# Three edits to a one-core transformer kernel: the last square of a norm added by VectorE, both tiles of a convolution in step, an output gate tile moved behind the pool projection

## Chip, cores and metric

The kernel runs on one core of one Trainium2 chip. The metric is the device time of one execution in microseconds; lower is better. The engines are called as in the profile: PE (TensorE), DVE (VectorE), ACT (ScalarE), POOL (GpSimd) and SP (SyncE, which here only issues the weight transfers).

## The reference, cut to what matters

A first block runs twice over 512 tokens of width 1024: a norm, one wide projection, a Fourier mix and a retention of four heads, then a feed-forward part with a convolution. A second block follows once, with a context of 256 tokens of its own (`xc`). Its parts in the order of the reference:

```python
x  = ada_out(x,  swiglu(ada_in(x,  mod,  0, norm_pre[0]), ffn_w_in[0], ffn_w_out[0]), mod,  0, norm_post[0], 0.5)
xc = ada_out(xc, swiglu(ada_in(xc, modc, 0, norm_pre[0]), ffn_w_in[0], ffn_w_out[0]), modc, 0, norm_post[0], 0.5)
p  = ada_in(x,  mod,  1, norm_pre[1]) @ w_in        # u, v, output gate, gates, pool
pc = ada_in(xc, modc, 1, norm_pre[1]) @ w_in[:, :M_COLS]
u = silu(short_conv(p[..., :512], conv_w, conv_b))  # three taps along the tokens
h_lat, h_ctx = mlstm_bidir(...)                     # q, k from u by head; chunks of 128; both directions
mix = concat([mlstm_out(h_lat, output_gate, head_norm), pool_mixer(p[..., M_COLS:], pool_w, pool_scale)])
x = ada_out(x, mix @ w_out, mod, 1, norm_post[1], 1.0)
x = ada_out(x, swiglu(ada_in(x, mod, 2, ...), ...), mod, 2, norm_post[2], 0.5)
```

Each `ada_in`, `ada_out`, the closing norm of the first block and each retention head hold an RMS norm: the mean of squares over the 1024 (or 256) features, plus eps, to the power -1/2, times the values. `mlstm_out` multiplies by the sigmoid of the output gate, `pool_mixer` subtracts a group of the pool projection from its moving mean and multiplies by a 128x128 weight.

## The kernel before

Activations lie with the features on the 128 partitions and the tokens along the free axis: a tile of `x` is 128x512, one of the context 128x256, eight tiles (`t` = 0 to 7) make the width. Every product in full precision is three matmuls of halves (`L400` high by high, `L401` low by high, `L402` high by low), so both operands need a high and a low part. ACT makes the high part (`high`, L1087: a copy that rounds), DVE the low one (`low` L1671 or `low_of` L1675: value minus high part).

**Weights** come in chunks of 128x1024 (eight 128x128 blocks). SP brings a chunk to `stage`, ACT makes `WH` (L1067), DVE makes `WL` (L1629), PE uses the eight blocks. `weights(name)` on ACT and DVE makes the chunks up to two beyond the one that `name` uses; `WH` and `WL` have three buffers, and the `WH` of a chunk waits until PE has finished the chunk three before it. A block is three matmuls.

**Norms.** ACT squares a tile (`square`, L1097 for the first into `SSQ`, L1100 for the others into `SCR`), DVE (or POOL for some norms) adds each square to `SSQ` (`add_square`, L1684), and PE sums over the partitions by `rms_first`: four tiny matmuls for 512 tokens from `SSQ` (L500) and four from the last square, which nobody has added, from `SCR` (L504). The records count a 4-byte matmul of this kind as two instructions, so that the trace shows x8. DVE adds eps (L1692), POOL takes the power (L2321), `rms_last` on PE spreads the result over the partitions (L510), and DVE multiplies (L1705), with ACT and DVE making high and low parts of the product.

**Order.** Each engine's program is one list written by hand, and engines wait for each other by semaphores. Some work is written as generators "behind" a linear layer: after every block of a long linear layer each engine calls `walk.tick()`, and `walk.pace` says how many calls make one step of the generator (`yield` to `yield`). In the output gate stage (`og`, four tiles of 128 output features, one chunk each) and in the one that follows (`v2x`, eight) the steps are given by hand: `BESIDE_OG` and `BESIDE_V2`.

**The second block's middle**, in the order of PE: `swiglu` of the context, first half (`c,0`), and of `x` first half, then the second half of the context (`c,1`, 2328 to 2438 us, with the norms `("ao",0,0)` and `("an",1,0)` behind it), output gates (`og`), the value projection `v2x`, the convolution's input `uc` (four heads; the context tile `uc` is 256 tokens, the `x` tile `ux` 512), gates, `v2c`, the pool projection `pu`, then `pool_mean(g)` (a 512x512 matrix of means), `pool_out(g)` and `q_and_k(h, which)`, and `scores(0,0)`. For the convolution ACT scales and adds the bias (`Identity`, L1447), DVE adds the two outer taps (L2157, L2160), ACT takes silu (L1450) and the high part, DVE the low part. DVE also makes `gates_sum`, `gates_maximum` and `gates_order` (L2120 to L2136) between heads.

## Time and profile before

| | |
|---|---|
| median of 3 runs (lowest, highest) | 3179.95 us (3179.87, 3182.98) |
| profiled execution: its own time, span | 3180.08 us, 3178.3 us |
| PE busy, share of the span, matmuls | 3069.9 us, 97%, 14914 |
| DVE busy | 1778.7 us, 56% |
| ACT busy | 1125.9 us, 35% |
| POOL busy | 144.8 us, 5% |
| mean granted clock of PE | 0.987 |
| weight transfers to `stage` | 533 of 512 KB, 3.3 us to landing each |

The profile is of one execution; a row's time is from the span's start. The granted clock is a share of full speed: 1.00 is 2.4 GHz and 0.50 is 1.2 GHz. A wait in brackets is the idle time of that engine just before the instruction, with what released it.

### The profile page before, as it was taken

How to read it: one execution, taken by the hardware profiler on the slowest of the kernel's cores; microseconds unless marked ns; L12 is line 12 of the kernel's file. 1: busy time of each engine (PE TensorE's matmuls, PEld its weight loads, DVE VectorE, ACT ScalarE, POOL GpSimd, SP SyncE). 2: the span in 40 equal slices, each digit the busy share in tenths (PEclk: the TensorE clock that was granted, in tenths of full speed). 3: DMA queues.
4: the chain of work that ended last, by engine and by line, in shares of the span. 5: the costliest groups of instructions: out<-in, count | busy, mean ns of one | idle time of the engine just before them, and what ended most of it. 6: DMA issues, size and time to landing. Idle time of an engine off the chain costs nothing. (4 is left out here: it accounts for less than half of the span.)

```text
span 3178.3 us, 36249 instructions
## 1 busy us (share of the span) xinstructions
PE 3069.9 (97%) x14914; PEld 2569.4 (81%) x14914; DVE 1778.7 (56%) x2524; ACT 1125.9 (35%) x1644; POOL 144.8 (5%) x129
## 2 busy tenths in 40 slices
PE   7999999999999999999999999999999989899998
PEld 5888888888778888888888889888898756778886
DVE  6566656766767566656755555323366655353234
ACT  3323332442324232333433434222234446332221
POOL 0001000000000001100000000000010004100000
PEclk9999999999999999999999999999999989999999
DMA  7354446443343343345322334222344130122221
GB/s 260 126 173 157 155 137 193 133 152 128 126 138 100 126 131 113 112 150 175 118 101 94 100 121 162 95 100 93 99 133 135 67 119 1 54 67 99 98 95 67
DMA packets 106916, 381.73 MB, mean 120 GB/s; under 512 B 11868, under 2 KB 13276, under 8 KB 106752
## 3 DMA queue, kind: packets, MB, share of 16 engines
q1 hardware_dynamic: 82992, 294.41, 27.8%
q10 hardware_dynamic: 23760, 85.01, 8.1%
q8 instruction: 118, 1.93, 0.2%
q14 instruction: 46, 0.38, 0.0%
HBM read 377.28 MB, written 2.10 MB: 119 GB/s over the span
## 5 line engine op out<-in xcount | busy, mean ns | idle before, releaser
L1629 DVE TENSOR_TENSOR WL<-stage,WH 128x1024 fp32r<-128x1024 f32 x533 | 655.8, 1234 | 674.7 <-ACT WH L1067 674.3
L400 PE MATMUL ps<-HH,WH 128*128 128x512 f32 x2188 | 858.1, 392 | 14.8 <-DVE HL L1671 5.8
L401 PE MATMUL ps<-HL,WH 128*128 128x512 f32 x2188 | 853.7, 390 | 0.0
L402 PE MATMUL ps<-HH,WL 128*128 128x512 f32 x2188 | 853.3, 390 | 0.0
L1067 ACT ACTIVATE WH<-stage 128x1024 fp32r<-128x1024 f32 x533 | 557.0, 1050 | 334.5 <-PE ps L402 325.5
L400 PE MATMUL ps<-GH,WH 128*128 128x512 f32 (+1 forms) x1652 | 587.5, 356 | 11.7 <-DVE WL L1629 5.7
L401 PE MATMUL ps<-GL,WH 128*128 128x512 f32 (+1 forms) x1652 | 584.9, 354 | 0.0
L402 PE MATMUL ps<-GH,WL 128*128 128x512 f32 (+1 forms) x1652 | 584.7, 354 | 0.0
L400 PEld LDWEIGHTS ps<-HH,WH 128*128 128x128 f32 x2188 | 412.3, 188 | 103.4 <-issue 8.3
L402 PEld LDWEIGHTS ps<-HH,WL 128*128 128x128 f32 x2188 | 412.0, 188 | 86.5
L401 PEld LDWEIGHTS ps<-HL,WH 128*128 128x128 f32 x2188 | 412.4, 188 | 82.4
L1087 ACT ACTIVATE GH<-SCR 128x512 fp32r<-128x512 f32 (+5 forms) x310 | 165.9, 551 | 700.9 <-DVE SCR L2041 232.9
L400 PEld LDWEIGHTS ps<-GH,WH 128*128 128x128 f32 x1652 | 313.5, 190 | 61.0 <-issue 7.1
L401 PEld LDWEIGHTS ps<-GL,WH 128*128 128x128 f32 x1652 | 313.6, 190 | 43.8
L402 PEld LDWEIGHTS ps<-GH,WL 128*128 128x128 f32 x1652 | 313.4, 190 | 43.0
L1671 DVE TENSOR_TENSOR GL<-SCR,GH 128x512 fp32r<-128x512 f32 (+1 forms) x214 | 133.1, 628 | 127.5 <-ACT GH L1087 127.5
L1656 DVE CUSTOM_DVE_ANT_0 MST<-MST,CB,PAR 128x1024 f32<-128x1024 f32 x158 | 201.9, 1279 | 0.9 <-ACT CB L1389 0.8
L2321 POOL TENSOR_TENSOR V<-V,HM 128x4 f32<-128x4 f32 (+1 forms) x26 | 30.1, 1156 | 2165.4 <-DVE V L1692 2165.4
L2340 POOL TENSOR_TENSOR GL<-SCR,GH 128x512 fp32r<-128x512 f32 (+3 forms) x80 | 89.8, 1145 | 771.2 <-ACT GH L1087 771.0
L2041 DVE TENSOR_TENSOR SCR<-ps,SCR 128x512 f32<-128x512 f32 (+1 forms) x66 | 39.6, 600 | 116.8 <-PE ps L402 112.0
L400 PE MATMUL ps<-WH,HH 128*128 128x256 f32 (+1 forms) x320 | 98.8, 309 | 4.0 <-DVE SCR L1837 4.0
L402 PE MATMUL ps<-WH,HL 128*128 128x256 f32 (+1 forms) x320 | 97.4, 304 | 0.0
(210 smaller groups left out, 2774.1 us busy)
## 6 DMA issues: line engine op xcount, KB each, us to landing
stage<-ws SPq DMA_DIRECT2D x533, 512.0 KB, 3.3
MST<-wm ACTq DMA_DIRECT2D x154, 512.0 KB, 3.3
Z<-wm SPq DMA_DIRECT2D x10, 512.0 KB, 6.8
TAB<-consts ACTq DMA_DIRECT2D x7, 448.0 KB, 3.5
MST<-wm SPq DMA_DIRECT2D x6, 512.0 KB, 6.3
out<-X SPq DMA_DIRECT2D x8, 256.0 KB, 2.1
X<-xT ACTq DMA_DIRECT2D x4, 256.0 KB, 5.4
X<-xT SPq DMA_DIRECT2D x4, 256.0 KB, 6.5
```

Of the source, the lines that this page charges most:

```text
L400: e.matmul(o, wh, mh, start=start, stop=False)
L401: e.matmul(o, wh, ml, start=False, stop=False)
L402: return e.matmul(o, wl, mh, start=False, stop=stop)
L1067: e.activation(wh, src, ACT.Copy).then_inc(whi.sem, whi.up(("w", i)))
L1087: e.activation(dst, src, ACT.Identity if "bias" in more else ACT.Copy, **more).then_inc(hi.sem, hi.up(name))
L1629: e.tensor_tensor(wl, src, wh.bitcast(F32), ALU.subtract).then_inc(wlo.sem, wlo.up(("w", i)))
L1656: e.tensor_tensor_reduce(out=products, in0=a, in1=b, scale=1.0, scalar=res if i else bias, op0=ALU.mult, op1=ALU.add, accum_out=res).then_inc(
L1671: e.tensor_tensor(dst, src, high_part.bitcast(F32), ALU.subtract).then_inc(lo.sem, lo.up(name))
L2041: made(e.tensor_tensor(T, bank("sb", who, half, jj)[:, 0:n], T, ALU.mult), "sb", who, half, jj)
L2321: e.tensor_tensor(V4[:, 4:4 + nt], V4[:, 0:nt], HM[:, 0:nt], ALU.pow).then_inc(power.sem, power.up((k,)))
L2340: e.tensor_tensor(dst, src, high_part.bitcast(F32), ALU.subtract).then_inc(plo.sem, plo.up(name))
```

## The change

1. **Last square by VectorE.** For every norm that is not in the new set `IN_TURN` (three heads of the retention in each of the two layers, and seven norms of the second block and its entry: 13 in all) the last square is also added to `SSQ` by the adding engine, and PE sums `SSQ` alone: one set of tiny matmuls in place of two. For `("an",0,0)` POOL adds it, for the others DVE.
2. **Steps.** Each generator of a norm has one more `yield`, `walk.pace` goes from (2, 3) to (3, 4), and `BESIDE_OG` and `BESIDE_V2` change.
3. **An output gate tile moved.** The fourth `og` tile, with its weight chunk and its sigmoid, stands behind the pool projection. `q_and_k(0, 0)` comes ahead of the first pool mean, and each `pool_out` one mean later. The blocks around it fall into chunks differently: there are 535 chunks, not 533; ACT also loads its table twice more (sigmoid, then exp).
4. **Convolution in step.** Both tiles of a head go through each step together: two `Identity`, then the taps of both, then silu and high part of both, then both low parts; the gates' steps on DVE stand behind the taps.

```diff
 
+                if k not in IN_TURN:
+                    pe.wait_ge(*added_by(k, last))
+                    stat_free()
+                    for t in range(n // 128):
+                        inst = e.matmul(STAT[:, t:t + 1], SSQ[:, t * 128:t * 128 + 128], OC[:, oc:oc + 1], start=True, stop=True)
+                    done(inst, ("ss", k))
+                    return
                 pe.wait_ge(*(added_by(k, last - 1) if last > 1 else (sq, "sq", k, 0)))
...
                 walk.need("mod", 0, 3 * j + 1)
+                yield
                 warm(alone)
                 rms_first(k, n, 0, 7)
...
             walk.behind.append(closing_norm())
-            walk.pace = (2, 3)
+            walk.pace = (3, 4)
...
             pe.wait_ge(lo, "h", ("an", 1, 0), 7)
-            for h in range(NH):
+
+            def output_gate(h):
                 p = take_bank(("og", h), ev, "og", h)
                 lin(("og", h), 8, lambda k: ("w_in2", 0, k * 128, 1024 + h * 128), hx, p[:, :], bg=False)
+
+            for h in range(3):
+                output_gate(h)
                 for _ in range(BESIDE_OG[h]):
                     walk.advance()
 
...
                     running_max(0, k // 2 - 2)
-            close()
+
+            output_gate(3)
 
             qk_w = {}
...
 
             pe.wait_ge(lo, "u", 3, 1)
             pe.wait_ge(lo, "v2", 1)
+            q_and_k(0, 0, score_bank("qk", 0, 0))
+            close()
             pool_mean(0)
-            q_and_k(0, 0, score_bank("qk", 0, 0))
-            pool_out(0)
             q_and_k(0, 1, score_bank("qk", 0, 1))
             q_and_k(0, 2, score_bank("qk", 0, 2))
             pool_mean(1)
+            pool_out(0)
+            pool_mean(2)
             pool_out(1)
-            pool_mean(2)
             pool_mean(3)
             pool_out(2)
             scores(0, 0)
...
                 else:
-                    T = take(("sq", k, t), *((mm, "ss", k) if t == (1 if k[0] == "r" else 7) else added_by(k, t)))
+                    T = take(("sq", k, t), *((mm, "ss", k) if k in IN_TURN and t == (1 if k[0] == "r" else 7) else added_by(k, t)))
...
             for h in range(NH):
                 weights(("uc", h))
-                for part, (name, n, a) in enumerate((("ux", S, h * 768 + 256), ("uc", C, h * 768))):
+                parts = (("ux", S, h * 768 + 256), ("uc", C, h * 768))
+                for part, (name, n, a) in enumerate(parts):
                     T = take((name, h), lo, "u", h, part)[:, 0:n]
                     act.wait_ge(mm, "uc", h)
                     e.activation(T, bank(name, h)[:, 0:n], ACT.Identity, scale=par("cw2", 4 + h),
                                  bias=par("cb2", h)).then_inc(ev.sem, ev.up((name, h)))
+                for part, (name, n, a) in enumerate(parts):
+                    T = SA(name, h)[:, 0:n]
                     act.wait_ge(dv, name, h)
                     e.activation(T, T, ACT.Silu).then_inc(ev.sem, ev.up(("silu", h, part)))
                     act.wait_ge(ev, "silu", h, part)
...
+
+            def last_square(k, n):
+                if k not in IN_TURN and added_by(k, 7)[0] is ssq:
+                    add_square(k, 7, n)
 
...
                         made(e.tensor_tensor(T, bank("y", l, h, t)[:, :], T, ALU.mult), "y", l, h, t)
+                    if h + 1 < NH:
+                        add_square(("r", l, h), 1, S)
 
...
             for h in range(NH):
                 weights(("uc", h))
-                if h == 1:
-                    gates_sum()
-                elif h == 2:
-                    gates_maximum()
-                elif h == 3:
-                    gates_order()
-                for part, (name, n, a) in enumerate((("ux", S, h * 768 + 256), ("uc", C, h * 768))):
+                parts = (("ux", S, h * 768 + 256), ("uc", C, h * 768))
+                for part, (name, n, a) in enumerate(parts):
                     T, p = SA(name, h), bank(name, h)
                     dve.wait_ge(ev, name, h)
                     made(e.scalar_tensor_tensor(out=T[:, 1:n], in0=p[:, 0:n - 1], scalar=par("cw2", h), in1=T[:, 1:n],
...
                     made(e.scalar_tensor_tensor(out=T[:, 0:n - 1], in0=p[:, 1:n], scalar=par("cw2", 8 + h), in1=T[:, 0:n - 1],
                                                 op0=ALU.mult, op1=ALU.add), name, h)
+                if h == 1:
+                    gates_sum()
+                elif h == 2:
+                    gates_maximum()
+                elif h == 3:
+                    gates_order()
+                for part, (name, n, a) in enumerate(parts):
+                    T = SA(name, h)
                     low(UL[:, a:a + n], T[:, 0:n], UH[:, a:a + n], "u", h, part)
             gates_last()
...
             root(("fin",), S)
-            for t in range(1, DT - 1, 2):
+            for t in range(1, DT, 2):
...
 
-        BESIDE_OG = [1, 1, 4, 4]
-        BESIDE_V2 = [1, 0, 1, 2, 2, 2, 1, 1]
+        BESIDE_OG = [2, 4, 5]
+        BESIDE_V2 = [1, 1, 1, 2, 2, 2, 1, 1]
         NORMS = [("n1", 0), *[("r", 0, h) for h in range(NH)], ("n2", 0),
                  ("n1", 1), *[("r", 1, h) for h in range(NH)], ("n2", 1),
                  ("an", 0, 1), ("fin",), ("an", 0, 0), ("ao", 0, 0), ("an", 1, 0), ("ao", 0, 1), ("an", 1, 1),
                  *[("hn", h) for h in range(NH)], ("ao", 1, 0), ("an", 2, 0), ("ao", 2, 0)]
+
+        IN_TURN = {("n1", 0), ("n1", 1), ("n2", 0), ("n2", 1), ("ao", 1, 0), ("an", 2, 0), ("ao", 2, 0),
+                   ("r", 0, NH - 1), ("r", 1, NH - 1)}
         FIRST_SQUARE = {k: before for before, k in zip(NORMS, NORMS[1:])}
         SLOTS_FREE = {("c", 0): ("dn", 1, 1, 7), ("x", 0): ("sd", "c", 0, 7), ("x", 1): ("sd", "x", 0, 7),
                       ("c", 1): ("sd", "x", 1, 7), ("y", 0): ("sum", 3, 5, 1), ("y", 1): ("sd", "y", 0, 7)}
```

(left out: the same edits of `closing_norm`, `ada_in` and `ada_out` for ACT and DVE, where the DVE version calls `last_square(k, n)` ahead of the new `yield`; and the reordering of the pool stage on ACT and DVE, which is that of PE.)

**DVE in the convolution.** DVE's rows of the head `h` = 1, first before, then of the changed kernel (L1629 is L1657 there, L2157 and L2160 are L2192 and L2195, L1671 is L1699; GT are the gates). 128x511 are the taps of `ux`, 128x255 those of `uc`.

```order
L1629 TENSOR_TENSOR WL<-stage,WH 128x1024
L2120 SCALAR_TENSOR_TENSOR GT<-GT 36x768
L2122 SCALAR_TENSOR_TENSOR GT<-GT 36x768
L2157 SCALAR_TENSOR_TENSOR SCR<-ps,PAR,SCR 128x511
L2160 SCALAR_TENSOR_TENSOR SCR<-ps,PAR,SCR 128x511
L1671 TENSOR_TENSOR GL<-SCR,GH 128x512
L2157 SCALAR_TENSOR_TENSOR SCR<-ps,PAR,SCR 128x255
L2160 SCALAR_TENSOR_TENSOR SCR<-ps,PAR,SCR 128x255
L1671 TENSOR_TENSOR GL<-SCR,GH 128x256
```

```order
L1657 TENSOR_TENSOR WL<-stage,WH 128x1024
L2192 SCALAR_TENSOR_TENSOR SCR<-ps,PAR,SCR 128x511
L2195 SCALAR_TENSOR_TENSOR SCR<-ps,PAR,SCR 128x511
L2192 SCALAR_TENSOR_TENSOR SCR<-ps,PAR,SCR 128x255
L2195 SCALAR_TENSOR_TENSOR SCR<-ps,PAR,SCR 128x255
L2160 SCALAR_TENSOR_TENSOR GT<-GT 36x768
L2162 SCALAR_TENSOR_TENSOR GT<-GT 36x768
L1699 TENSOR_TENSOR GL<-SCR,GH 128x512
L1699 TENSOR_TENSOR GL<-SCR,GH 128x256
```

The four taps now follow the weight chunk directly, the two gate instructions stand between them and the low parts, and the two low parts are last.

**ACT in the output gate stage.** Z<-ps is the sigmoid of an `og` tile, SCR<-TAB a square of the context for `("an",1,1)`, WH a weight chunk; before, then changed (L1423 is L1440 there, L1067 is L1083, L1097 and L1100 are L1113 and L1116).

```order
L1423 ACTIVATE Z<-ps 128x512
L1067 ACTIVATE WH<-stage 128x1024
L1423 ACTIVATE Z<-ps 128x512
L1067 ACTIVATE WH<-stage 128x1024
L1097 ACTIVATE SSQ<-TAB 128x256
L1100 ACTIVATE SCR<-TAB 128x256 x2
L1423 ACTIVATE Z<-ps 128x512
L1067 ACTIVATE WH<-stage 128x1024
L1100 ACTIVATE SCR<-TAB 128x256 x5
L1423 ACTIVATE Z<-ps 128x512
L1067 ACTIVATE WH<-stage 128x1024 x2
```

```order
L1440 ACTIVATE Z<-ps 128x512
L1083 ACTIVATE WH<-stage 128x1024
L1113 ACTIVATE SSQ<-TAB 128x256
L1116 ACTIVATE SCR<-TAB 128x256
L1440 ACTIVATE Z<-ps 128x512
L1083 ACTIVATE WH<-stage 128x1024
L1116 ACTIVATE SCR<-TAB 128x256 x6
L1440 ACTIVATE Z<-ps 128x512
L1083 ACTIVATE WH<-stage 128x1024 x2
```

The same eight squares stand one output gate tile earlier, since there are three tiles and not four.

**ACT in the pool stage**, from the high parts of the pool projection on. HH<-ps with PAR is a pool output, HH<-ps without it a pool mean, the single GH<-ps are parts of q and k; before, then changed.

```order
L1087 ACTIVATE GH<-ps 128x512 x4
L1067 ACTIVATE WH<-stage 128x1024 x2
L1087 ACTIVATE HH<-ps 128x512
L1067 ACTIVATE WH<-stage 128x1024
L1087 ACTIVATE GH<-ps 128x512
L1087 ACTIVATE HH<-ps,PAR 128x512
L1087 ACTIVATE GH<-ps 128x512
L1087 ACTIVATE GH<-ps 128x256
```

```order
L1103 ACTIVATE GH<-ps 128x512 x4
L1083 ACTIVATE WH<-stage 128x1024
L1440 ACT_TABLE_LOAD
L1440 ACTIVATE Z<-ps 128x512
L1083 ACTIVATE WH<-stage 128x1024
L1103 ACTIVATE GH<-ps 128x512
L1083 ACTIVATE WH<-stage 128x1024 x2
L1103 ACTIVATE HH<-ps 128x512
L1083 ACTIVATE WH<-stage 128x1024
L1103 ACTIVATE GH<-ps 128x512
L1103 ACTIVATE GH<-ps 128x256
```

A table load, the sigmoid of the fourth output gate tile and the first part of q stand ahead of the first pool mean; the first pool output is no longer between the parts of q and k.

## Rows read from the trace of the kernel before

**Rows 1.** Busy time by engine in four stages of the second block

```profile
core 0: us, PE busy (x) PEld busy (x) DVE busy (x) ACT busy (x) POOL busy (x), PEclk, DMA share, GB/s
2328.00:2438.00 110.00, 100.94 (x807) 99.63 (x806) 77.08 (x104) 50.56 (x76) 9.27 (x6) 0.96 0.47 156
...
2496.00:2561.00 65.00, 55.35 (x271) 45.95 (x270) 40.40 (x58) 28.99 (x41) 0.00 (x0) 0.89 0.21 72
...
2613.00:2720.00 107.00, 93.97 (x459) 62.08 (x458) 57.21 (x120) 64.31 (x147) 50.20 (x51) 0.95 0.01 2
...
2580.36:2612.63 32.27, 22.80 (x76) 16.61 (x76) 22.67 (x28) 21.34 (x31) 0.00 (x0) 0.84 0.49 157
```

**Rows 2.** Timeline of PE: waits in these stages, wait in brackets

```profile
start us, us, engine line op out<-in xcount [idle before <-releaser]
2376.89 1.02 PE L500 MATMUL ps<-OC,SSQ 128*128 128x1 f32 x8 [1.84 <-DVE SSQ L1684]
...
2438.16 0.79 PE L400 MATMUL ps<-HH,WH 128*128 128x512 f32 x1 [4.71 <-DVE HL L1675]
...
2536.01 0.79 PE L400 MATMUL ps<-WH,GH 128*128 128x512 f32 x1 [4.29 <-DVE WL L1629]
...
2546.86 0.80 PE L400 MATMUL ps<-WH,GH 128*128 128x512 f32 x1 [5.36 <-DVE WL L1629]
...
2583.77 0.77 PE L400 MATMUL ps<-WH,GH 128*128 128x512 f32 x1 [3.41 <-DVE GL L1671]
```

**Rows 3.** Same view as rows 1, short stretches; and one wait elsewhere

```profile
2378.00:2384.80 6.80, 6.80 (x34) 6.80 (x34) 3.44 (x6) 1.43 (x3) 1.02 (x1) 0.50 0.40 124
...
2535.00:2541.80 6.80, 5.49 (x12) 3.80 (x12) 5.33 (x9) 2.08 (x4) 0.00 (x0) 0.50 0.24 77
...
2582.80:2589.60 6.80, 5.83 (x14) 4.66 (x15) 3.08 (x4) 1.99 (x3) 0.00 (x0) 0.50 0.24 77
...
891.00:904.00 13.00, 9.63 (x43) 7.68 (x42) 10.30 (x17) 4.11 (x5) 0.00 (x0) 1.00 0.52 170
...
894.73 0.51 PE L400 MATMUL ps<-GH,WH 128*128 128x512 f32 x1 [3.37 <-DVE GL L1671]
```

**Rows 4.** Timeline of PE and DVE around the norm of a retention head

```profile
288.35 0.95 PE L500 MATMUL ps<-OC,SSQ 128*128 128x1 f32 x8
289.17 1.03 PE L504 MATMUL ps<-OC,SCR 128*128 128x1 f32 x8
290.06 0.36 PE L400 MATMUL ps<-WH,HH 128*128 128x256 f32 x1
...
284.45 1.28 DVE L1874 TENSOR_TENSOR SCR<-ps,SCR 128x512 f32<-128x512 f32 x2
285.77 1.23 DVE L1629 TENSOR_TENSOR WL<-stage,WH 128x1024 fp32r<-128x1024 f32 x1
289.70 1.22 DVE L1629 TENSOR_TENSOR WL<-stage,WH 128x1024 fp32r<-128x1024 f32 x1 [2.71 <-ACT WH L1067]
```

**Rows 5.** One head of the convolution: engines, and a wait of ACT

```profile
2524.60:2534.74 10.14, 7.12 (x38) 5.78 (x36) 7.22 (x10) 4.17 (x8) 0.00 (x0) 1.00 0.16 52
...
2519.78 0.63 ACT L1450 ACTIVATE SCR<-SCR 128x512 f32<-128x512 f32 x1 [4.70 <-DVE SCR L2160]
```

**Rows 6.** Timeline of ACT, DVE, PE at the output gate stage's end

```profile
2465.93 1.04 ACT L1067 ACTIVATE WH<-stage 128x1024 fp32r<-128x1024 f32 x1
...
2465.27 0.42 DVE L1684 TENSOR_TENSOR SSQ<-SSQ,SCR 128x256 f32<-128x256 f32 x1 [0.20 <-ACT SCR L1100]
2467.01 1.22 DVE L1629 TENSOR_TENSOR WL<-stage,WH 128x1024 fp32r<-128x1024 f32 x1 [1.31 <-ACT WH L1067]
...
2466.39 0.50 PE L500 MATMUL ps<-OC,SSQ 128*128 128x1 f32 x4
```

**Rows 7.** Timeline of ACT: a table load and what follows

```profile
2501.53 1.28 ACT L1438 ACT_TABLE_LOAD   x1
2502.83 0.84 ACT L1438 ACTIVATE GT<-GT 36x768 f32<-36x768 f32 x1
```

## Prediction before the run

> **What bounds the kernel now.** I read the windows by stage first. PE is busy for 97% of the span (front table), so an edit gains only where PE stands idle, runs at half clock, or has instructions taken away. The stages that the change touches hold much of such time [rows 1]: 9.1 us idle in the context's second half (`c,1`, 110.00 less 100.94), 9.7 in the convolution (65.00 less 55.35), 9.5 in the 32.27 us from the end of the pool projection to the first scores, 13.0 in the head stage behind it. The granted clock there is 0.96, 0.89, 0.84 and 0.95, where the span's mean is 0.987. PE's timeline shows five waits and their releasers [rows 2]: 1.84 us for the last added square, 4.71 for the low part of `h` ahead of the output gates, 4.29 and 5.36 for `WL` chunks in and behind the convolution, 3.41 for the low parts of the pool projection. Behind such waits stand 6.8 us at 0.50 clock, with PE busy 6.80, 5.49 and 5.83 us in three of them [rows 3]. At half clock half of that work is lost time: 3.4, 2.7 and 2.9 us. A wait does not always bring that: one of 3.37 us elsewhere lies in a stretch at 1.00 [rows 3].
>
> **Last square, retention heads.** Between two starts the second set of tiny matmuls takes 290.06 - 289.17 = 0.89 us of a PE that never waits there [rows 4]. Six heads: +5.3 us. In exchange DVE makes six adds of 0.64 us (half of the 1.28 for two tensor operations of that size). The add comes directly behind L1874, which ends at 285.73, so it is done near 286.4, and PE wants it at 288.35: 1.9 us of cover. `WL` behind it slides by 0.64 us; DVE then idles 2.71 us before the next chunk, so nothing else moves. Bounds: 4.9 to 5.3.
>
> **Last square elsewhere.** The closing norm saves the same 0.89, the context's `("an",0,1)`, with half the matmuls, 0.4: +1.3 (0.9 to 1.3). The other norms stand in stages that DVE and ACT chain, below.
>
> **`c,1`.** The 1.84 us wait for the sum, the second set, and the half clock of 3.4 us behind it [rows 2, 3] could together give 6. But from there to 2438 PE goes at the pace of the squares, affines and `WL` on DVE (77.08 us busy of 110.00), and the 4.71 us wait at the end is for the last of the affines: what PE wins early it waits longer there. The extra `yield`, the new pace and one more add on DVE pull steps together by some blocks and no more. Bounds 0 and +6; I take +2.5, nearer to none because the end wait stands.
>
> **Output gates and `v2x`.** With three tiles in place of four the same eight squares of the context lie one tile (24 products) earlier on PE, and the sum of `("an",1,1)` needs the last of them added by DVE. Before, the add of t = 6 ended at 2465.69, PE came at 2466.39 and did not wait [rows 6]. After, PE's sum comes about 3 us earlier, near 2463.3 in the old time, and DVE's add of t = 7 is queued behind the `WL` whose `WH` comes behind the third sigmoid. In the old time that ends near 2466.1, with the `WH` duration of 1.04 and `WL` of 1.22: a new wait of 2.8 us, less 1.1 for steps taken earlier, and a half-clock stretch worth up to 3.4, of which I take 2.0 by the two cases of rows 3. Together -3.7 (bounds -5.5 and 0, where the clock stays and the wait is covered).
>
> **Convolution.** One head takes 10.14 us, DVE is busy 7.22 of them [rows 5]. Its 2.9 us idle are three waits: for silu and high part of `ux`, the same for `uc`, and `WH`. ACT for its part waits 4.70 us for the taps, because the gates stand ahead of them. After, the gates' work covers the silu waits, the taps of both tiles run together, and only about 0.5 remains: a period of 7.7 us, 2.4 us less, over three heads with 7.3 in all. The last chunk's `WL`, which releases PE at 2536.01 after 4.29 us, then comes before PE wants it: that wait and its 2.7 of half clock vanish, 7.0 us. `WL` for the second wait is made some 8.1 us earlier (7.3, and 0.8 in the last head) while PE comes 7.0 earlier: 5.36 becomes 4.2, and its half clock stays. Sum +8.1, bounds 5 (half clock stays once more) and 10.
>
> **Pool stage.** The 24 products of the fourth output gate tile, now behind the pool projection, fill the 3.41 us wait for its low parts [rows 2]; the work itself is only moved. Pool outputs one mean later no longer wait for high and low part of their own mean. I laid out the three engines' new rows with the old durations and found six waits of 0.4 to 2.2 us, 6.7 in all, the largest where four `WH`, a table load of 1.28 and the last outputs meet on ACT. Before it was 9.5 idle: +2.8. The clock of 0.84 over 32.27 us means 10.3 us at half clock; at the busy share of rows 3 (5.83 of 6.80) 4.4 us were lost. If it stays full: +4.4. Together +7.2. Bounds: 3 (half clock remains) and 9. Two more table loads: the trace has 1.28 us for a load, and the next instruction starts 1.30 after its start [rows 7]; one hides while PE does the moved tile, the other is in my 6.7. The Trainium skill has a dearer price: "ScalarE: Activation LUTs", What ACT_TABLE_LOAD costs, gives about 2.66 us for every switch, nearly half of it a drain behind the load. By that the gain would be 2.8 us smaller; the trace of before shows no such gap.
>
> **Head stage.** Two more chunks cost 1.04 on ACT and 1.22 on DVE each [rows 6]. One lies in the head stage, where PE waits for these engines (93.97 busy of 107.00): -1.0 (-0.5 to -1.2).
>
> **Sum.** 5.3 + 1.3 + 2.5 - 3.7 + 8.1 + 7.2 - 1.0 = 19.7. From the profiled execution's 3180.08 that is 3160.4; the median of the runs is 0.13 lower: **3160.2 us**, 0.6% less.
>
> **Rivals.**
> 1. *More.* The clock stays full in `v2x` (+2), `c,1` gives 6 (+3.5), conv and pool reach 10 and 9 (+3.7): about 3151. For it: the wait of 3.37 without a fall. Against: the 4.71 and 4.2 waits remain.
> 2. *Half of it.* `c,1` gives nothing, `v2x` -5.5, the pool stage 3 since short waits hold the clock down, the rest as forecast: 3160.2 + 2.5 + 1.8 + 4.2 = 3169. A rule in the skill speaks for this: "TensorE: Matmul & The Clock Gate", Part 1, says that the throttled clock is the default and activity releases it, so many small waits might do what one long one did. The trace has 1.84 us in front of one such stretch, and none at 3.37.
> 3. *No change.* As 2, and the convolution gives 5, and `v2x` loses its wait and the full 3.4, the order of chunks in the pool stage costing its 2.8 of idle: 3169 + 3.1 + 1.4 + 2.8 = 3176. For it: PE is 97% busy, so waits tend to be met again later.
> 4. *Slower.* The retention sum now waits for DVE. If a head's add falls behind the next `WL` (289.70 to 290.92), PE waits until 291.6 in place of 288.35, 3.3 us, and runs 6.8 us at half clock, 3.4 more: six times 6.7 is 40, giving 3200. It decides once the add ends later than 288.35; rows 4 leave 1.9 us and show L1874 directly ahead, so only a head with a different order would do it.
> 5. *Table loads at the page's price.* The drain would stand on ACT where PE waits for it: 3160.2 + 2.8 = 3163. No row bears it out.
>
> **How the numbers follow.** The forecast, 3154 to 3165, has 0.55 (rival 5 in it with 0.04); rival 1 0.13; rival 2 0.19; rival 3 0.08; rival 4 with other losses 0.05. A measurement here tells 0.2%, 6.4 us, from no change: rivals 1 and 2 are faster by more. So faster 0.87, same 0.08, slower 0.05. The bounds of all terms added up give gains of 31 and 8 (3149 and 3172); 3149 to 3173 leaves out rivals 3 and 4 and the ends of 1 and 2, about 0.2.
>
> **What would show it.** L504 gone from six heads, and PE's L500 there without a wait. WL to WL in the convolution 7.7 us, no wait of PE before the last head's chunk, about 4 us at the next. 29 to 31 us from the moved tile to the first scores with a clock near 1.00. A new wait of PE for L500 near the start of `v2x`, of 2 to 3 us. The 4.71 us wait still there. It would be wrong if the heads' sums wait for DVE, if a period of the convolution stays above 9 us, or if the clock in the pool stage stays at 0.84.

## The result and the profile after

The changed kernel takes 3161.22 us (median of 4 runs, 3160.31 to 3165.75) where the kernel before took 3180.55 us beside it (3179.87 to 3182.98). The ratio is 0.994, 95% interval 0.9925 to 0.9955: faster by 0.6%, 14 to 24 us. The forecast was 3160.2 in a range of 3149 to 3173. The profiled execution has a time of 3160.31 us, the shortest of the four. One execution, in experiment 12, ran slow (4367.79 us, mean granted clock 0.651), and no ratio includes it.

The page's head for the changed kernel: span, and PE's busy time, share and instructions.

```profile
span 3158.5 us, 36112 instructions
...
PE 3052.7 (97%) x14822; PEld 2553.0 (81%) x14822; DVE 1785.3 (57%) x2538; ACT 1130.7 (36%) x1648; POOL 145.1 (5%) x130
```

PE has 92 matmul records fewer, which are the 46 tiny matmuls, and is busy 17.2 us less (3069.9 before), partly because it runs at half clock less (mean granted clock 0.989, 0.987 before).

Windows of the changed kernel: the context's second half from its first chunk to the first output gate (beside the first row of [rows 1]), one head of the convolution (beside [rows 5]), the stretch from the end of the pool projection to the first scores (beside the last of [rows 1]), and the 13 us around the wait of 3.37 us in the first block (beside [rows 3]).

```profile
core 0: us, PE busy (x) PEld busy (x) DVE busy (x) ACT busy (x) POOL busy (x), PEclk, DMA share, GB/s
2330.42:2430.59 100.17, 91.38 (x759) 90.56 (x757) 75.37 (x103) 49.21 (x73) 8.35 (x6) 1.00 0.51 164
...
2509.65:2517.34 7.69, 7.69 (x46) 6.68 (x45) 7.04 (x10) 4.17 (x7) 0.00 (x0) 1.00 0.20 68
...
2561.68:2592.51 30.83, 25.14 (x99) 18.24 (x98) 24.28 (x30) 25.87 (x36) 0.00 (x0) 0.94 0.61 204
...
891.00:904.00 13.00, 9.64 (x36) 7.83 (x36) 9.20 (x13) 4.22 (x5) 0.00 (x0) 0.87 0.47 151
```

Read against the rows before: a head of the convolution takes 7.69 us (10.14, [rows 5]) with DVE busy 7.04 of them; the pool stretch takes 30.83 us with the output gate tile inside it (32.27 without, [rows 1]) at a clock of 0.94 (0.84). The last row is a stretch that the change does not touch. It has 0.87 where [rows 3] have 1.00.

PE's timeline of the changed kernel at the places of [rows 2 to 4, 6]:

```profile
290.66 0.95 PE L501 MATMUL ps<-OC,SSQ 128*128 128x1 f32 x8
291.47 0.36 PE L400 MATMUL ps<-WH,HH 128*128 128x256 f32 x1
...
894.38 0.50 PE L400 MATMUL ps<-GH,WH 128*128 128x512 f32 x1 [3.36 <-DVE GL L1699]
...
2366.47 0.36 PE L400 MATMUL ps<-GH,WH 128*128 128x256 f32 x1 [1.87 <-DVE WL L1657]
...
2430.59 0.65 PE L400 MATMUL ps<-HH,WH 128*128 128x512 f32 x1 [4.71 <-DVE HL L1703]
...
2457.80 0.35 PE L501 MATMUL ps<-OC,SSQ 128*128 128x1 f32 x2 [2.59 <-issue]
...
2528.34 0.79 PE L400 MATMUL ps<-WH,GH 128*128 128x512 f32 x1 [3.98 <-DVE WL L1657]
...
2588.07 0.77 PE L400 MATMUL ps<-HH,WH 128*128 128x512 f32 x1 [2.25 <-DVE HL L1699]
...
2592.51 0.51 PE L400 MATMUL ps<-GH 128*128 128x512 f32 x1 [1.54 <-DVE SCR L2260]
```

The sum of a retention head is one set, and the next product starts 0.81 us after it (1.71 before, [rows 4]: 290.06 - 288.35). The 1.84 us wait of [rows 2] for the last added square is gone, but a wait of 1.87 us for a `WL` chunk stands earlier in the same stage. The 4.71 us wait ahead of the output gates is as it was. The first wait in the convolution (4.29 us) is gone, the second is 3.98 (5.36, [rows 2]). A new one of 2.59 us stands in front of the sum of the context's last norm. The profile names "issue" as its releaser; DVE's timeline tells what it was.

```profile
287.37 0.68 DVE L1906 TENSOR_TENSOR SCR<-ps,SCR 128x512 f32<-128x512 f32 x1
287.97 0.69 DVE L1712 TENSOR_TENSOR SSQ<-SSQ,SCR 128x512 f32<-128x512 f32 x1
288.57 1.22 DVE L1657 TENSOR_TENSOR WL<-stage,WH 128x1024 fp32r<-128x1024 f32 x1
...
2456.06 1.22 DVE L1657 TENSOR_TENSOR WL<-stage,WH 128x1024 fp32r<-128x1024 f32 x1 [1.31 <-ACT WH L1083]
2457.28 0.42 DVE L1712 TENSOR_TENSOR SSQ<-SSQ,SCR 128x256 f32<-128x256 f32 x1
```

First group: the add of a head's last square directly behind L1906 and ahead of `WL`, done at 288.66, two microseconds before PE asks. Second group: the add of the context's last square at 2457.28 stands behind a `WL` chunk and ends at 2457.70; PE starts at 2457.80. ACT's timeline around the two new table loads of the pool stage:

```profile
2564.72 1.28 ACT L1440 ACT_TABLE_LOAD   x1
2567.14 0.60 ACT L1440 ACTIVATE Z<-ps 128x512 f32<-128x512 f32 x1 [1.13 <-PE ps L402]
...
2587.14 1.28 ACT L1530 ACT_TABLE_LOAD   x1
2588.44 1.33 ACT L1530 ACTIVATE SCR<-Z,GC 128x512 f32<-128x512 f32 x2
```

**Where the time went.** Both traces cut at the same places (starts of the same weight chunk on DVE up to the fifth row's end, then PE's starts behind the waits named in the table):

| stretch | before, us | after, us | gain | forecast |
|---|---|---|---|---|
| start to the ninth chunk | 76.23 | 78.57 | -2.3 | 0 |
| retention, layer 0 | 346.38 | 343.64 | 2.7 | 2.65 |
| first block between its retentions | 604.14 | 605.81 | -1.7 | 0 |
| retention, layer 1 | 316.47 | 313.77 | 2.7 | 2.65 |
| to the end of the halves of `c,0` and `x` | 990.34 | 988.63 | 1.7 | 1.3 |
| context's second half | 104.60 | 100.17 | 4.4 | 2.5 |
| output gates to the second wait (2546.86, 2528.34) | 108.70 | 97.75 | 11.0 | 4.4 + tile |
| from there to the first scores (2612.63, 2592.51) | 65.77 | 64.17 | 1.6 | 7.2 - tile |
| scores to the end | 565.65 | 565.97 | -0.3 | -1.0 |
| sum | 3178.28 | 3158.48 | 19.8 | 19.7 |

The moved tile is 24 products at 0.229 us, 5.5: it leaves the seventh stretch and enters the eighth. Without it these gained 5.5 and 7.1. The two stretches that lost 4.0 us contain nothing of the change; more on them below. Each stretch also holds the stretches at half clock of this one execution, and these differ between executions of the same code. The experiments' profiles say how much where they run a stretch unchanged; for the pool stage and the last stretch it is several us.

### The profile page after: what moved, and what is told of

Its sections match the earlier page's. It is cut to its first block and busy times, and to the rows that moved or that the text cites. A ratio compares the mean times of both kernels' runs of the same rounds, so it can differ in the third digit from the quotient of the medians.

```text
span 3158.5 us, 36112 instructions
## 1 busy us (share of the span) xinstructions
PE 3052.7 (97%) x14822; PEld 2553.0 (81%) x14822; DVE 1785.3 (57%) x2538; ACT 1130.7 (36%) x1648; POOL 145.1 (5%) x130
## 5 line engine op out<-in xcount | busy, mean ns | idle before, releaser
L1657 DVE TENSOR_TENSOR WL<-stage,WH 128x1024 fp32r<-128x1024 f32 x535 | 657.4, 1231 | 671.7 <-ACT WH L1083 671.4
L1083 ACT ACTIVATE WH<-stage 128x1024 fp32r<-128x1024 f32 x535 | 559.5, 1050 | 342.9 <-PE ps L402 331.5
L1699 DVE TENSOR_TENSOR GL<-SCR,GH 128x512 fp32r<-128x512 f32 (+1 forms) x214 | 133.3, 630 | 118.6 <-ACT GH L1103 118.5
```

The lines of the kernel that those rows point to most:

```text
L1083: e.activation(wh, src, ACT.Copy).then_inc(whi.sem, whi.up(("w", i)))
L1657: e.tensor_tensor(wl, src, wh.bitcast(F32), ALU.subtract).then_inc(wlo.sem, wlo.up(("w", i)))
L1699: e.tensor_tensor(dst, src, high_part.bitcast(F32), ALU.subtract).then_inc(lo.sem, lo.up(name))
```

## Experiments

Times are medians; each ratio is to runs of the kernel before on the same chip, with its 95% interval. "Kernel before with" means one part alone; "changed kernel with" means one part undone or altered.

**1. Retention heads alone.** Kernel before with the last square of six heads added by DVE:

```diff
...
+                    if h + 1 < NH:
+                        add_square(("r", l, h), 1, S)
...
+        IN_TURN = {k for k in NORMS if not (k[0] == "r" and k[2] < NH - 1)}
```

(left out: PE's single set and ACT's wait, as in the change.)

> The kernel before with one edit alone: the last square of three heads in each retention layer is added by VectorE, and PE sums SSQ alone. My theory: each of the six sums takes 0.8 to 0.9 us less on PE and PE does not wait for the add, so the head's period falls from 58.5 to 57.6 us and the whole gains 5.3 us (about 3175). Rival: the 0.64 us add pushes the next WL and the gain is given back there: periods stay near 58.3, gain under 2 us.

Measured: 3176.75 us, ratio 0.9983 (0.9974 to 0.9991), 5.4 us less. Two heads take 115.17 us between the same two chunks of DVE (116.93 before), 57.6 each, as said. The term of 5.3 stands.

**2. and 3. How late may the add be?** The changed kernel with the add behind one, and behind both, of the `WL` chunks that follow it:

```diff
                     if h + 1 < NH:
+                        weights(("v", l, h + 1), ahead=1)
                         add_square(("r", l, h), 1, S)
```

```diff
-                        part_b(h + 1, lambda: rms_first(("r", l, h), S), lambda: part_e(h))
+                        part_b(h + 1, lambda: (add_square(("r", l, h), 1, S), rms_first(("r", l, h), S)), lambda: part_e(h))
```

> The changed kernel with one WL chunk of DVE put ahead of the last square's add in the six retention heads. My theory: the add slides by 1.2 us and the cover is 1.9, so PE's sum still starts without a wait and the time is that of the changed kernel within 1 us. Rival: the cover is not there, and each head shows a wait of 0.5 us or more (3 us in all, and more where the clock falls).

Measured: 3164.65 us, ratio 0.9937 (0.9922 to 0.9951), that of the changed kernel. DVE, then PE, in one head:

```profile
287.45 1.22 DVE L1657 TENSOR_TENSOR WL<-stage,WH 128x1024 fp32r<-128x1024 f32 x1
288.59 0.68 DVE L1712 TENSOR_TENSOR SSQ<-SSQ,SCR 128x512 f32<-128x512 f32 x1
```

```profile
290.03 0.95 PE L501 MATMUL ps<-OC,SSQ 128*128 128x1 f32 x8
```

The add ends at 289.27 and PE starts its sum at 290.03 with no bracket: no wait. The cover of 1.9 us was real.

> The changed kernel with the add behind both WL chunks, the case of my rival for a slower kernel. My theory: PE waits 3.3 us at each of six sums, 20 us in all, and the clock falls behind some of these waits (3.4 us each where it falls): 20 to 40 us slower than the changed kernel. Rival: the wait is met by slack later in the head (scores on POOL and DVE), then less than 12 us.

Measured: 3198.50 us, ratio 1.0043 (1.0028 to 1.0058), which is slower than the kernel before. DVE, PE, and PE's chain of waits (line waited for, total us, times, longest):

```profile
289.65 1.23 DVE L1657 TENSOR_TENSOR WL<-stage,WH 128x1024 fp32r<-128x1024 f32 x1 [2.69 <-ACT WH L1083]
290.80 0.69 DVE L1712 TENSOR_TENSOR SSQ<-SSQ,SCR 128x512 f32<-128x512 f32 x1
```

```profile
291.54 1.11 PE L501 MATMUL ps<-OC,SSQ 128*128 128x1 f32 x8 [3.07 <-DVE SSQ L1712]
```

```profile
PE ps L501 <- DVE SSQ L1712: 18.4, 6, 3.1
PE ps L501 <- issue: 2.6, 1, 2.6
```

Six waits of 3.07 make 18.4 us. Against the changed kernel the ratios are 0.0103 apart, 33 us, and in the traces the two retentions are 33.5 us longer. The other 14 or so fit the half clock: the trace has a stretch of it at each of the six waits, 3.4 or 6.8 us long. So the place of one 0.69 us instruction decides whether this kernel is 0.6% faster than before or 0.4% slower. The forecast's price (40 us against 33 measured) was of the right size.

**4. Convolution alone**, kernel before with part 4; **5.** the same, but with the gates ahead of the taps as before:

```diff
                 weights(("uc", h))
+                if h == 1:
+                    gates_sum()
...
                 parts = (("ux", S, h * 768 + 256), ("uc", C, h * 768))
```

> The kernel before with the convolution's part alone (both tiles in step, gates behind the taps). My theory: WL to WL 7.1 to 7.7 us for the first heads, the wait of 4.29 us and its half clock gone, the second wait about 4; gain 8.1 us (about 3172). Rival: the chunk of the last head is late for another reason (its transfer or WH), so that PE waits as long as before and the gain is under 3 us.

> The kernel before with both tiles of the convolution in step, but the gates still ahead of the taps. My theory: WL to WL about 8.5 us (10.14 before, 7.7 with the gates behind), the first wait gone, the second 6 us or so: gain 5 of the 8. Rival: the gates' place is what counts, then the period stays above 9.5 and the gain is under 3.

Measured: 3173.50 us, ratio 0.9967 (0.9954 to 0.9979) for part 4; 3178.78, ratio 0.9983 (0.9974 to 0.9993) with the gates first. Two successive `WL` chunks of DVE, in step with the gates behind, then with the gates first:

```profile
2521.06 1.21 DVE L1632 TENSOR_TENSOR WL<-stage,WH 128x1024 fp32r<-128x1024 f32 x1
2528.74 1.21 DVE L1632 TENSOR_TENSOR WL<-stage,WH 128x1024 fp32r<-128x1024 f32 x1
```

```profile
2522.10 1.23 DVE L1632 TENSOR_TENSOR WL<-stage,WH 128x1024 fp32r<-128x1024 f32 x1 [0.53 <-ACT WH L1067]
2530.47 1.23 DVE L1632 TENSOR_TENSOR WL<-stage,WH 128x1024 fp32r<-128x1024 f32 x1 [0.52 <-ACT WH L1067]
```

7.68 us apart and 8.37 apart, from 10.14. The stretch from the first output gate to the wait behind the convolution (108.70 before) is 100.18 us in the one and 100.93 in the other: 8.5 and 7.8 won. But its first part, up to the `WL` chunk ahead of the first taps, has the same code in both and took 0.6 us less in the second, where the half clock after the 4.7 us wait was shorter. From that chunk on the two took 31.60 and 32.94 us (40.05 before): 8.5 and 7.1 won. So the taps together do most of it, and the place of the gates is worth 1.3 us, by which the wait that is left is longer (5.31 us against 3.97). For the second I had expected a period of 8.5 and a gain of 5: the period holds. For the gain the stretch says 7.1, and the times say 2 to 8, which leaves 5 open. Its rival is refuted by the period. The medians lie 5 us apart, but the intervals overlap, and the profiled execution of the second (3173.54) is 5 us under its own median, so I go by the parts of the traces that the edit touches.

**6. and 7. The moved tile.** Kernel before with the tile and the pool order (part 3), and with the tile alone:

```diff
+            output_gate(3)
...
+        BESIDE_OG = [1, 4, 5]
```

> The kernel before with the fourth output gate tile behind the pool projection and each pool output a mean later, the other parts left out. My theory: from the end of the pool projection to the first scores 37.8 us with the tile counted in before, 31 now, gain 7; one more chunk in the head stage costs 0.7; the sum of the context's last norm is taken in turn, so PE has no wait of 2.6 us there; net gain near 6 us (about 3174). Rival: the gain in the combined kernel came from the clock by chance, and here the stage takes 34 us or more.

> The kernel before with the fourth output gate tile behind the pool projection, but pool outputs and means in the old order. My theory: the 3.41 us wait and the half clock behind it go (6 us), while the waits of 0.4 to 2.4 us for pool means stay: gain near 5 after 0.7 for the chunk. The order of outputs is worth the rest, 1 to 2 us. Rival: the order does most of it, and this kernel gains under 3 us.

Measured: 3182.73 us, ratio 1.0005 (0.9996 to 1.0014), and 3181.23, ratio 0.9996 (0.9987 to 1.0005). Neither has a gain that the times can show. The trace of part 3 alone, in windows: first the 6.8 us at the new wait, then output gates to the second wait of the convolution, then from there to the first scores.

```profile
2467.80:2474.60 6.80, 6.49 (x19) 5.51 (x20) 1.59 (x4) 1.49 (x3) 0.71 (x1) 0.51 0.25 81
2442.91:2551.77 108.86, 96.85 (x457) 80.94 (x457) 62.51 (x104) 45.89 (x70) 4.56 (x6) 0.91 0.18 62
2551.77:2615.94 64.17, 57.37 (x233) 42.98 (x234) 34.22 (x40) 34.87 (x47) 0.00 (x0) 0.96 0.48 164
```

The last row less 5.5 for the tile is 58.7 against 65.77: 7.1 us won, as in the changed kernel (the tile alone wins 5.9 by the same two marks: 2546.49 to 2611.85). But the middle row plus 5.5 is 114.4 against 108.70: 5.7 us lost. PE's timeline shows by what:

```profile
2468.11 0.34 PE L500 MATMUL ps<-OC,SSQ 128*128 128x1 f32 x1 [2.34 <-DVE SSQ L1696]
```

This wait of 2.34 us did not exist before [rows 6], and the clock behind it is 0.51 for 6.8 us. I had expected none here, since the sum is "in turn", as before the change: PE sums `SSQ` and then the last square by a second set, so that DVE need not add the last one. But with only three tiles PE reaches the sum before DVE has added even the square before the last. So the mechanism is the missing tile, not the last square: taken away from the output gate stage, it no longer covers the context's norm. That stage pays for most of what the pool stage wins; in part 3's trace the last stretch, with its further chunk, is 1.4 us longer too (567.07 against 565.65). By itself the tile's move is worth nothing that the times show. My expectations of 6 and 5 were wrong.

**8. Seven norms back in turn.** Changed kernel with only the retention's last squares added by DVE:

```diff
...
+        IN_TURN = {k for k in NORMS if not (k[0] == "r" and k[2] < NH - 1)}
```

(left out: the set that it replaces, and POOL's last add.)

> The changed kernel with the seven norms outside the retention back to two sets of tiny matmuls (steps, yields and pace stay). It tells what the last square and what the steps did in the context's second half (4.5 us gained there in the changed kernel's profile, 2.5 forecast). My theory: the steps do most of it: this kernel keeps 3 of the 4.5 us; it loses 1.3 in the closing norm and the context's first norm and wins back the new wait of 2.59 us ahead of the sum of the context's last norm; in all within 1.5 us of the changed kernel. Rival: the single set of matmuls did it, then 1.8 us of wait for the sum come back and this kernel is 4 us slower than the changed one.

Measured: 3164.15 us, ratio 0.9942 (0.9929 to 0.9956). The context's second half takes 102.34 us here (100.17 changed, 104.60 before), with no half clock in PE's work in either of the two: half of that stage's gain, 2.2 us, is from the single set. The other half is not the steps alone. In the profile of the kernel before 6.8 us of the stage, ahead of its last wait, ran at half clock; in two other kernels where the stage has the code of before (experiments 5 and 7) it was 3.4 us, and the stage took 103.04 and 103.03. So 1.6 us of the other half hang on the length of one stretch at half clock, and no run has the steps alone. My theory's 3 of 4.5 was too much for the steps; the rival's "all" was wrong as well. From the first output gate to the second wait it takes 95.94 us against 97.75, as the wait ahead of the last norm's sum is gone.

**9. Only the last norm in turn**, changed kernel:

```diff
-                   ("r", 0, NH - 1), ("r", 1, NH - 1)}
+                   ("r", 0, NH - 1), ("r", 1, NH - 1), ("an", 1, 1)}
```

> The changed kernel with one norm, the context's last (behind the output gates), summed in turn again: two sets of two tiny matmuls, no add by DVE behind the WL chunk. My theory: the last add before it ends at 2454.75 and PE comes at 2455.2, so the wait of 2.59 us goes and 0.4 come back: the stretch from the first output gate to the chunk behind the convolution falls from 97.7 to about 95.9 us, and up to 1.8 more where the clock does not fall. Rival: PE waits for the square before that one instead, as in the kernel with the tile alone (2.34), and nothing is won.

Measured: 3157.91 us, ratio 0.9924 (0.9911 to 0.9936); the interval overlaps that of the changed kernel, so the gain is read from the trace. The stretch from the first output gate to the second wait is 94.85 us, 2.9 less. The sum has no wait any more, and what is left is POOL's power:

```profile
2460.69 0.38 PE L517 MATMUL ps<-IDN,V 128*128 128x128 f32 x1 [0.30 <-POOL V L2365]
```

**10. The 4.71 us wait, by tiles**, changed kernel:

```diff
-            pe.wait_ge(lo, "h", ("an", 1, 0), 7)
...
-                lin(("og", h), 8, ..., hx, p[:, :], bg=False)
+                lin(("og", h), 8, ..., hx, p[:, :], ready=(lambda k: ("h", ("an", 1, 0), k)) if h == 0 else None, bg=False)
```

> The changed kernel with PE's wait of 4.71 us ahead of the output gates taken apart: the first output gate's eight blocks wait for one tile of the normed x each, not for the last before the first. My theory: seven blocks (4.8 us of work) run inside the wait, it falls to under 0.5 us, and as DVE's chain of the context's norm does not come sooner, most of it returns as a longer wait for that norm's sum (2.59 becomes 5 or more): gain 1 to 3 us. Rival 1: the chain hangs on PE's steps, comes sooner with them, and 4.7 or more are won. Rival 2: all of it returns, nothing is won.

Measured: 3160.89 us, ratio 0.9930 (0.9918 to 0.9943). The wait is gone, and another stands at the context's first sum behind it:

```profile
2431.87 0.24 PE L501 MATMUL ps<-OC,SSQ 128*128 128x1 f32 x1 [2.54 <-DVE RC L2034]
...
2453.56 0.24 PE L501 MATMUL ps<-OC,SSQ 128*128 128x1 f32 x1 [2.60 <-issue]
```

From the first chunk of the context's second half (2328.17) to the wait behind the convolution it takes 194.33 us against 197.92: 3.6 won. Only 2.2 of them are the edit's: 4.71 us of waits went and 2.54 came. The other 1.4 fit the clock. Over the 6.8 us from the wait of 2.60 (2.59) us on, here and then in the changed kernel:

```profile
2453.56:2460.36 6.80, 6.80 (x34) 5.75 (x35) 2.65 (x5) 0.97 (x3) 1.62 (x1) 1.00 0.45 154
...
2457.80:2464.60 6.80, 6.80 (x27) 5.64 (x28) 2.30 (x5) 0.69 (x2) 1.62 (x1) 0.75 0.49 154
```

The rest did not go where I had said: 2.54 us now wait for the first of the two context norms, and the wait for the second is what it was. The profile names `RC` as the releaser, but DVE's add of that norm's last square stands directly behind it, and behind a `WL` chunk again, and ends at 2431.77, 0.10 before PE starts:

```profile
2430.13 1.22 DVE L1657 TENSOR_TENSOR WL<-stage,WH 128x1024 fp32r<-128x1024 f32 x1 [1.48 <-ACT WH L1083]
2431.27 0.16 DVE L2034 SCALAR_TENSOR_TENSOR RC<-MOD,PAR 128x8 f32<-128x8 f32 x1
2431.35 0.42 DVE L1712 TENSOR_TENSOR SSQ<-SSQ,SCR 128x256 f32<-128x256 f32 x1
```

**11. Gate copies behind a chunk**, changed kernel:

```diff
+            weights(("v2c",), ahead=0)
             gates_last()
```

> The changed kernel with the four last gate copies of DVE (1.75 us) put behind the first of the three WL chunks that they stood ahead of. My theory: PE's wait of 3.98 us behind the convolution falls to 2.2, gain 1.7 us, in a range too small for the times alone, so the trace decides. Rival: the transpose of the gates, which needs these copies, is then late, and 1.7 us come back there.

Measured: 3161.61 us, ratio 0.9938 (0.9925 to 0.9952). PE's wait behind the convolution:

```profile
2524.19 0.79 PE L400 MATMUL ps<-WH,GH 128*128 128x512 f32 x1 [2.22 <-DVE WL L1657]
```

2.22 us in place of 3.98, as said; the stretch is 1.7 shorter in the trace. The times can't show so little.

**12. The three together.**

> The changed kernel with the edits of the last three runs together: the context's last norm in turn, the first output gate by tiles, the gate copies behind a WL chunk. Measured by themselves against the changed kernel's trace they took 2.8, 3.6 and 1.7 us from the stretch that runs from the end of the context's half to the chunk behind the convolution. My theory: they lie at three different waits and add up, 7 to 8 us: about 3153, ratio to the kernel before 0.991 to 0.992. Rival: the chain of the context's norm on DVE sets the end of the output gate stage whatever PE does, so that the first two share one gain and the sum is 4 to 5: ratio 0.9925.

Measured: 3156.95 us (median of all five), ratio 0.9919 (0.9903 to 0.9934). The stretch of experiment 10 takes 192.28 us against 197.92: 5.6 won, less than the sum of 8.1 and more than the rival's 4 to 5. The waits do add up: 11.28 us in the changed kernel (4.71, 2.59, 3.98) are 4.76 here (2.54, 2.22), 6.5 less, which is 2.2, 2.6 and 1.8 of the three edits. The sum of 8.1 was too high by the 1.4 us of clock in experiment 10's share. By the trace of this stretch it beats the kernel before and the changed one; the times do not tell it apart from the changed kernel (0.9940, intervals overlap) or from experiment 9 alone (0.9924).

## Why the prediction was right

- **Retention heads**, +5.3: 5.4 in the table, 5.4 in experiment 1. That the add was covered by 1.9 us is shown by experiments 2 and 3.
- **Other norms**, +1.3: 1.7.
- **`c,1`**, +2.5 (0 to 6): 4.4. Mis-sized: I held that squares, affines (the multiply-adds that apply a norm) and `WL` on DVE set the pace, so that the 4.71 us wait would take back what PE won. It did not grow at all (4.71 in both), so the affines moved forward as far as PE did. The kernel before shows the same without any edit: with 3.4 us less at half clock (experiments 5 and 7) the stage took 1.6 us less and the wait was as long (4.72 and 4.73). The single set has 2.2 us of the 4.4 (experiment 8); the rest is steps and the half clock that the profile of before had here and the changed kernel's had not, and no run parts these two.
- **Output gates and `v2x`**, -3.7: 10.95 measured over the stretch, less 5.5 for the tile and 8.5 for the convolution by itself, leaves -3.1. Of that about +0.6 is a shorter half clock behind the 4.71 us wait in the changed kernel's profile (experiments 4 and 5 show such a difference on the same code). The wait was forecast as 2.8 and is 2.59. Its cause was told only half: in the changed kernel it is the add of t = 7 behind `WL`, but with fewer tiles PE would wait 2.34 us for the add before it too (experiments 6 and 7). In the changed kernel, whose steps come earlier, that wait does not show even where the sum is in turn (experiments 8 and 9).
- **Convolution**, +8.1: 8.5 by itself, of which 1.3 is the place of the gates. Period 7.7 forecast, 7.69 measured; second wait 4.2 and 3.98.
- **Pool stage**, +7.2: 7.1. The waits sum to 5.7 (30.83 less 25.14), not 6.7, and the clock did not stay full: 0.94. How much is the edit's is less sure than the figure. The pool stage of the kernel before, with its own code, took 65.77, 65.58 and 65.51 us in three profiles and 62.49 in a fourth, that of experiment 4, which had less half clock in it. Against the fourth the gain is 3.8 us.
- **Table loads**: a load takes 1.28 us and the next instruction starts 1.30 behind its start (2587.14 and 2588.44), on this very path. The drain of the Trainium skill's page "ScalarE: Activation LUTs" (What ACT_TABLE_LOAD costs) is not seen there; by its figures the next start would be 2.66 behind. The prediction called that drain nearly half of the price; the same section of the Trainium skill gives 1.38 us of 2.66, a little over half, and does not say on which side of the load it stands. There is none on either side here: ACT's instruction before ended 0.02 us before the load. And since the prediction has one of the two loads hidden, that price would have cost 1.4 us by its own sum, and not 2.8. The other load ended at 2566.00 and ACT then waited 1.13 us for PE.
- **Head stage**, -1.0: -0.3 over a longer stretch. The term is not shown: that stretch, unchanged from the changed kernel, took from 565.4 to 571.9 us in the profiles of experiments 2, 3 and 9 to 12, and the changed kernel's 565.97 is near the low end.
- **Slips in the sums.** The lower bounds of the terms add up to a gain of 7.1, not 8, which gives 3173, the upper end of the stated range. Rival 3 adds 1.4 us for `v2x` to rival 2's -5.5, but the whole wait and the full half clock, 2.8 and 3.4, are only 0.7 more than that.
- **Luck.** The terms missed by +0.1, +0.4, +1.9, +0.6, +0.4, -0.1 and +0.7, 4.0 in all in the kernel's favour. Two stretches that the change leaves alone lost 4.0 in the profiled execution and hid that. The start up to the ninth chunk varied between 75.3 and 78.8 us over the twelve experiments' profiles, and the first block between the retentions by a clock fall that comes or does not (604.1 us without, 605.7 to 606.0 with one of 3.4 us). The small error against the median is thus in part chance, and so is that of the terms for `c,1`, the pool stage and the head stage. The terms for the retention, the convolution's period and the waits that went or came do not depend on it.

## What to carry to other kernels

When work is moved to fill a wait, price the place that it leaves: there it covered someone too. Here a tile that won 7 us in the pool stage cost 5.7 where it had stood. In the changed kernel, whose steps come earlier, the cost was about 3, and with the last norm's sum in turn besides (experiment 9) next to nothing was left of it; no run has the changed kernel with the tile in its old place. When a sum is handed from PE to another engine, look at what is queued there between the last input and the moment PE asks: one chunk of cover was enough, two turned a gain into a loss. And stretches cut at the same instructions in both traces showed terms of 1 to 2 us, where medians could not tell 5 apart; but only where the half clock in them was the same or was counted as well, since the same code differed by 0.6, 1.6 and 3.3 us with it here.

## What the runs showed of the hardware

The same wait is followed by half clock in one execution and not in another. 3.37 us at 894.73 had 1.00 around it [rows 3]; 3.36 us at 894.38 in the changed kernel has 0.87 over the same 13 us, and the stretch of the table that holds it took 1.7 us longer, though nothing there was changed. Behind the wait of 2.34 us (experiment 6) the clock was 0.51 for 6.8 us. Behind the wait of 2.60 us it was 1.00 in experiment 10, and 0.75 behind the 2.59 us of the changed kernel. The spread of executions goes with it: in experiment 11 the shortest, 3155.36 us, has a mean granted clock of 0.992, the longest, 3165.45, one of 0.986. So a term "half clock behind this wait" should be held as a chance: none, about 1.6 us for a stretch of 3.4 us, or up to 3.4 us for one of 6.8. What decides it stays open here.
